# Twenty taps of the depthwise convolution moved to GpSimd, and a sample's rotated keys turned in one flip

## The reference

```
z = rmsnorm(h, ln_in) @ w_in            # c_q, c_kv, k_r, g_a, u_val, u_gate, g_c
s = (q_lat . ckv + q_rope . krope) * ATTN_SCALE        # cached and new keys
o_lat = softmax(s) @ ckv
u = u_val * sigmoid(u_gate)
v = causal_dwconv(concat([past, u]), conv_w, width 31) + bias
v = silu(layernorm(v))
h = h + concat([y_a, y_c]) @ w_out
h = h + sigmoid(rmsnorm(h, ln_pg) @ w_pg) * (p @ w_pe)
```

## Time and profile before

| | |
|---|---|
| median of 3 runs | 798.32 us (798.23 to 798.53) |
| the profiled execution's own time | 798.34 us |
| its span | 796.5 us |
| busy TensorE | 767.9 us |
| busy VectorE | 566.2 us |
| busy ScalarE | 411.7 us |
| busy GpSimd | 65.0 us |

### The profile page before, as it was taken

The page is one execution under the profiler, slowest core; times in us unless marked ns, Lnnn a source line. Parts: engine busy times, 40 slices in busy tenths (PEclk is TensorE's granted clock), DMA queues, the critical chain, the costliest instruction groups (busy, mean ns, idle before and its releaser), DMA issues.

```text
span 796.5 us, 10486 instructions
## 1 busy us (share of the span) xinstructions
PE 767.9 (96%) x3766; PEld 603.7 (76%) x3766; DVE 566.2 (71%) x1093; ACT 411.7 (52%) x942; POOL 65.0 (8%) x114
## 2 busy tenths in 40 slices
PE   6999999999999999999999999999999999999995
PEld 4799877767667578888888988776676756888874
DVE  3348989877877786545463799897878677656477
ACT  3565635654465472353465475457444657323554
POOL 5000123210000220000000011232000000000000
PEclk9999999999999999999999999999999999999998
DMA  8722222100000163422182323211100004341203
GB/s 293 219 72 84 81 69 83 38 27 27 27 1 28 45 206 120 134 80 80 53 259 62 92 88 86 53 57 28 53 14 14 14 14 145 109 144 53 90 17 132
DMA packets 45113, 65.54 MB, mean 82 GB/s; under 512 B 12510, under 2 KB 24634, under 8 KB 45046
## 3 DMA queue, kind: packets, MB, share of 16 engines
q1 hardware_dynamic: 41226, 58.45, 23.3%
q0 software_dynamic: 3776, 6.40, 2.7%
q10 hardware_dynamic: 60, 0.02, 0.0%
HBM read 57.87 MB, written 7.18 MB: 82 GB/s over the span
## 4 chain that ended last, share of the span: by engine, by line
PE 84%; DVE 8%; ACT 5%; issue 2%; DMA 1%; SPq 0%; ACTq 0%; DVEq 0%
PE acc L628 18%; PE acc L630 18%; PE acc L629 18%; PE sharedT L562 4%; PE acc L748 4%; PE sharedT L810 3%; PE sharedS L823 3%; PE sharedO L837 3%; PE sharedS L562 2%; PE sharedO L562 2%; DVE WLO L1379 1%; ACT WHI L1003 1%; DVE VT L1444 1%; PE sharedS L796 1%; PE sharedS L797 1%
## 5 line engine op out<-in xcount | busy, mean ns | idle before, releaser
L628 PE MATMUL acc<-WHI,XHI 128*128 128x512 f32 (+1 forms) x710 | 309.0, 435 | 0.9 <-DVE XLO L1389 0.9
L630 PE MATMUL acc<-WHI,XLO 128*128 128x512 f32 (+1 forms) x710 | 275.3, 388 | 0.0
L629 PE MATMUL acc<-WLO,XHI 128*128 128x512 f32 (+1 forms) x710 | 274.7, 387 | 0.0
L1444 DVE SCALAR_TENSOR_TENSOR VT<-UX,CWT,VT 128x640 f32<-128x640 f32 x240 | 211.8, 883 | 5.4
L628 PEld LDWEIGHTS acc<-WHI,XHI 128*128 128x128 f32 x710 | 133.9, 189 | 33.8 <-issue 8.6
L1379 DVE SCALAR_TENSOR_TENSOR WLO<-WR,GT,WHI 128x512 fp32r<-128x512 f32 (+1 forms) x142 | 98.6, 736 | 82.6 <-ACT WHI L1003 82.2
L629 PEld LDWEIGHTS acc<-WLO,XHI 128*128 128x128 f32 x710 | 134.2, 189 | 30.5 <-issue 8.6
L630 PEld LDWEIGHTS acc<-WHI,XLO 128*128 128x128 f32 x710 | 133.6, 188 | 26.4
L1003 ACT ACTIVATE WHI<-WR,GT 128x512 fp32r<-128x512 f32 (+1 forms) x142 | 93.5, 710 | 95.9 <-PE acc L630 90.9
L1196 ACT ACTIVATE SB<-SB,NBIAS 128x384 f32<-128x384 f32 (+1 forms) x80 | 45.7, 572 | 39.3 <-DVE NBIAS L1500 39.0
L837 PEld LDWEIGHTS sharedO<-V,PT 128*128 128x128 f32 x320 | 44.5, 191 | 16.1 <-issue 8.8
(11 more groups left out here) (207 smaller groups left out, 839.7 us busy)
## 6 DMA issues: line engine op xcount, KB each, us to landing
WR<-in_w_in_dram SPq DMA_DIRECT2D x32, 256.0 KB, 3.0
WR<-in_w_in_dram SPq DMA_DIRECT2D x16, 512.0 KB, 3.7
WR<-in_w_out_dram SPq DMA_DIRECT2D x16, 512.0 KB, 3.6
WR<-in_w_pg_dram SPq DMA_DIRECT2D x16, 512.0 KB, 3.6
WR<-in_w_in_dram SPq DMA_DIRECT2D x8, 416.0 KB, 3.4
residual_spill<-H SPq DMA_DIRECT2D x5, 512.0 KB, 4.1
H<-residual_spill SPq DMA_DIRECT2D x10, 256.0 KB, 3.3
H<-in_x_prompt_dram SPq DMA_DIRECT2D x4, 512.0 KB, 7.6
```

Of the source, the lines that this page charges most:

```text
L628: mm(out, hi, w_hi, start=(first and k == 0), stop=False)
L629: mm(out, hi, w_lo, start=False, stop=False)
L630: last = mm(out, lo, w_hi, start=False, stop=(final and k == 1))
L1444: ins = stt(out=out, in0=src, scalar=w, in1=out, op0=ALU.mult, op1=ALU.add)
```

## The change

Two edits that don't touch each other's data.

The first: of the channel tile c = 3, the taps 0 to 19 leave VectorE's list and go to GpSimd. VectorE keeps 104 taps per layer, 24 of them in the units. GpSimd does tap 0 in one instruction, and each of the other 19 in two, a product into a new tile TAPPED and a sum onto VT; each of them waits for the one before (`conv_pool`). They stand in its list after the SSUM loads and wait for ScalarE's copies of the tile. VectorE's tap (3, 20) waits for all 39 of them. The tuple of taps in the units is a new one, in which the first tap of tile 3 stands in unit 19.

The second: CKR holds the two key blocks side by side in its 128 columns, each twice, so that one flip turns both. `cache_out` copies the latents in one instruction and the two blocks of rotated keys in one each, from 64 partitions to 64 partitions. The zeros stand in CTK from the start instead of in CKR.

```diff
+POOL_TAPS = 20
+TAP_ORDER = [(c, k) for c in range(4) for k in range(TAPS) if c < 3 or k >= POOL_TAPS]
...
-for _u, _m in enumerate((1, 3, 3, 2, 0, 2, 3, 2, 1, 2, 3, 1, 1, 3, 3, 2, 1, 2, 0, 2, 2, 2, 1, 2)):
+for _u, _m in enumerate((0, 1, 1, 1, 0, 1, 1, 1, 1, 1, 1, 1, 1, 1, 1, 0, 0, 0, 0, 2, 2, 2, 2, 3)):
     TAP[NB + _u] = _take(_m)
...
-        CKR = sb("CKR", [P, CACHED, 2, 128])
+        CKR = sb("CKR", [P, CACHED, P])
+        TAPPED = sb("TAPPED", [P, TOK])
...
             src = a["cache_krope"][l, s].rearrange("(j p) r -> p j r", p=P)
+            dst = CKR[:, slot, :].rearrange("p (j k r) -> p k j r", j=2, k=2)
             for k in range(2):
-                lo = NOPE + ROPE * k
-                pool.dma_start(CKR[:, slot, :, lo:lo + ROPE], src).then_inc(cache_in[slot], 16)
+                pool.dma_start(dst[:, k], src).then_inc(cache_in[slot], 16)
...
                 for j in range(2):
                     flip(quad(name)[:, j, :], CKV[:, slot, j, :])
-                    last = flip(quad(name)[:, 2 + j, :], CKR[:, slot, j, :])
-                fill_inc(last, (l, name))
+                fill_inc(flip(quad(name)[:, 2, :], CKR[:, slot, :]), (l, name))
...
-                drain_inc(copy(CTK[:, :, 0:PAST], bank((l, name))[:, :].rearrange("p (a k) -> p a k", a=2)), (l, name))
+                copy(CTK[:, 0, 0:PAST], bank((l, name))[:, 0:PAST])
+                for j in range(2):
+                    out = copy(CTK[NOPE:P, 1, P * j:P * (j + 1)], quad(name)[NOPE * j:NOPE * (j + 1), 2, :])
+                drain_inc(out, (l, name))
...
-                        dve.wait_ge(conv_done, CONVS * l + TAP_AT[c, k - 1] + 1)
+                        if (c, k) == (3, POOL_TAPS):
+                            dve.wait_ge(conv_pool, (2 * POOL_TAPS - 1) * (l + 1))
+                        else:
+                            dve.wait_ge(conv_done, CONVS * l + TAP_AT[c, k - 1] + 1)
...
-            nc.gpsimd.memset(CKR[:, :, :, 0:NOPE], 0.0).then_inc(const_set, 1)
-            nc.gpsimd.memset(CTK[0:NOPE, 1, PAST:], 0.0).then_inc(const_set, 1)
+            nc.gpsimd.memset(CTK[0:NOPE, 1, :], 0.0).then_inc(const_set, 1)
...
+            c, steps = 3, (2 * POOL_TAPS - 1) * l
+            copied_wait(pool, (l, ("u", c, 0)))
+            copied_wait(pool, (l, ("u", c, 1)))
+            out = VTv[:, :, c, :].rearrange("p t (b j) -> p t b j", j=NS)
+            product = TAPPED[:, :].rearrange("p (t b j) -> p t b j", t=TILES, j=NS)
+            for k in range(POOL_TAPS):
+                w = CWT[:, c, k:k + 1]
+                src = UX[:, c % 2, :, k:k + NS].rearrange("p (t b) j -> p t b j", t=TILES)
+                if k == 0:
+                    nc.gpsimd.tensor_scalar(out, src, w, GT[:, l, G_CB + c:G_CB + c + 1],
+                                            ALU.mult, ALU.add).then_inc(conv_pool, 1)
+                else:
+                    pool.wait_ge(conv_pool, steps + 2 * k - 1)
+                    nc.gpsimd.tensor_scalar(product, src, w, None, ALU.mult).then_inc(conv_pool, 1)
+                    pool.wait_ge(conv_pool, steps + 2 * k)
+                    nc.gpsimd.tensor_tensor(out, out, product, ALU.add).then_inc(conv_pool, 1)
```

More of the change, by code:

```diff
@@ L74 @@
          (0, 2), ("x", 3, 1), (1, 1), ("x", 4, 0), (0, 3), ("x", 4, 1), (1, 2), (0, 4), (1, 3), (1, 4)]
-TAP_ORDER = [(c, k) for c in range(4) for k in range(TAPS)]
+POOL_TAPS = 20
+TAP_ORDER = [(c, k) for c in range(4) for k in range(TAPS) if c < 3 or k >= POOL_TAPS]
 TAP_AT = {x: i for i, x in enumerate(TAP_ORDER)}
@@ L293, in build @@
         conv_done = sem("conv_done")
+        conv_pool = sem("conv_pool")
         ln_done = sem("ln_done")
@@ L856, in tensor_layer @@
                 pe.wait_ge(tables_in, 16 * 2)
-                pe.wait_ge(const_set, 10)
+                pe.wait_ge(const_set, 9)
             for t in range(TILES):
@@ L1448, in vector_layer @@
             if l == 0:
-                dve.wait_ge(const_set, 10)
+                dve.wait_ge(const_set, 9)
             taps("z5")
@@ L1752, in pool_start @@
             nc.gpsimd.memset(SMASK[:, 2, 128:240], NEG).then_inc(const_set, 1)
-            nc.gpsimd.memset(CTK[0:NOPE, 1, PAST:], 0.0).then_inc(const_set, 1)
+            nc.gpsimd.memset(CTK[0:NOPE, 1, :], 0.0).then_inc(const_set, 1)
             nc.gpsimd.memset(MASK[:, :], 0.0).then_inc(const_set, 1)
-            pool.wait_ge(const_set, 9)
+            pool.wait_ge(const_set, 8)
             nc.gpsimd.memset(MASK[0:P // 2, 512 - P // 2:512], NEG).then_inc(const_set, 1)
```

## The result

The changed kernel takes 830.11 us (median of 4 runs, 828.94 to 832.13) beside 798.42 us for the kernel before: 4.0% slower, with an interval of the ratio from 1.0379 to 1.042. I had forecast slower, 809.1 us, with a range that ended at 819. The time lies outside it.

The account below looks back on a forecast made before the run. TensorE's own work and short waits were taken to bound the kernel. From 798.34 us, flips -1.5, relief -1.0, third tap +1.6 and blocking +11.7 gave +10.8, so 809.1 us, range 796.5 to 819.

Parts of the forecast that it names:

- What bounds the kernel: Whole kernel: TensorE, busy 96% of the span; time changes only where it has fewer instructions or waits less.
- One flip fewer: Samples' attention: eight flips fewer save 0.88 us per layer, 0.1 lost to ScalarE's copies; -1.5 us in all.
- Relief: Units: VectorE without 20 taps shortens TensorE's waits by 0.5 us per layer, -1.0 us in all.
- the third tap: Unit 23, end of the convolution: three taps instead of two delay TensorE by 0.8 us per layer, +1.6 us.
- The sum of the three terms: Flips -1.5, relief -1.0 and third tap +1.6 together: -0.9 us, giving 797.4 us without disturbance.
- How long GpSimd takes: GpSimd's chain: product 1.0 us, sum 1.6, 54 us per layer (29 to 67), ending at about 223.
- the limit at 62: Units: GpSimd's chain may take 62 us from its start, to about 231, before VectorE's tap (3, 20) is held up.
- GpSimd late: Rival at tap (3, 20): without blocking, the chain ends at 236 and VectorE stands 5 us; 807.4 us, chance 0.08.
- Blocking: Units: GpSimd's reads hold up VectorE's low parts and a gate, 5.85 us per layer, +11.7 us; chance 0.52.
- the four low parts: Units, 169 to 229 us: two VectorE instructions each, before masks for which TensorE's scores already wait; 0.65 us per instruction.
- the lateness: Tap (3, 20): a GpSimd chain late under blocking, nothing in the sum, up to 5 us per layer for the range.
- the slot: When VectorE reaches tap (3, 20): 228.87, moved by blocked low parts to 232.8, with slack 234.8.

Follow-up runs that it names:

- e9: One-flip edit alone on the kernel before, first scores matmul waiting for the latents' copy only, sample 5's probabilities copied before the gate tiles: 796.86 us, ratio 0.9973.
- e12: Kernel before with only ScalarE's order in sample 5 changed, probabilities copied before the gate tiles: 797.81 us, ratio 0.9986.
- e4: Changed kernel, VectorE not waiting for GpSimd (its 11 taps of tile 3 kept apart, not added), GpSimd doing tap 0 alone: 799.69 us, ratio 1.0007.
- e3: Changed kernel, VectorE not waiting for GpSimd (its 11 taps of tile 3 kept apart, not added), GpSimd's work the same: 813.96 us, ratio 1.0191.
- e5: Changed kernel without VectorE's wait, GpSimd's 38 products and sums per layer replaced by 100 dependent memsets: 800.52 us, ratio 1.0018.
- e2: Changed kernel with GpSimd's product written as multiply, then add 0, instead of multiply alone: 817.44 us, ratio 1.0232.
- e11: Kernel before plus 32 dependent GpSimd instructions on idle tiles in the first layer, four of each form; instructions timed, no kernel time given.

## Why the prediction was wrong

- **What bounds the kernel:** right. TensorE's own work and its short waits set the time, and the loss is found again in TensorE's waits and the clock. The waits listed under the result grew by 28.8 us, the clock costs 2.7, the flips give 1.8 back: 29.7 of 30.6 us between the two profiled executions.
- **One flip fewer, -1.5 us:** TensorE does save about 0.88 per layer (scores of the later samples start 5.36 us apart instead of 5.49), but the price of the copies was mis-sized: 1.1 us per layer instead of 0.1. I looked only at the wait for the copies and took for granted that the others were ahead. In sample 5 ScalarE has no gap from the cache copy to the probabilities, so what the copies take more in front is waited for behind, with the flip saved coming on top. Net +0.2 per layer, and -0.58 once the waits are mended (e9 against e12).
- **Relief, -1.0, and the third tap, +1.6:** the third tap measured 0.8 us per layer (L568, 1.6 in two waits). The units, from their first scores to the first flip of the convolution, take 82.8 us in the kernel before (162.03 to 244.82) and in e4 (163.71 to 246.54), although e4 has 0.73 us of wait for that tap. So relief was worth as much, 0.7 per layer where I took 0.5. The sum of the three terms, -0.9 us, was right within what can be measured (e4). That is partly luck, as it has errors of both signs in it: the flips gave nothing and relief gave more.
- **How long GpSimd takes:** here the prediction failed. "I take 1.0 and 1.6": the sum measured 1.53 undisturbed, the product 1.88, outside my bounds of 0.65 to 1.3. The bound rested on a memset and on the thought that streams pass one after another at its rate; that an instruction with less to do can take twice as long isn't in any row. The chain was 74.8 us instead of 54, with the limit at 62 (the 1.59 us per instruction there include the 0.1 between two).
- **The rival "GpSimd late"** (chance 0.08) is what happened: VectorE stood 12.3 us at tap (3, 20). I priced it at 5 us per layer without blocking. It came with blocking, and the two work together: by the runs, about 20.7 us for the length of the instructions, about 11.0 for what the chain grows beside VectorE's instructions.
- **Blocking, +11.7:** the mechanism is there, shown by e3 against e4 (14.3 us), and e5 binds it to what a memset doesn't do. Its size was too small even for durations as I had taken them. e2 comes near the case that I had described: its product and sum take 1.03 and 1.75 us on average, beside my 1.0 and 1.6, its chain ends at 225.8 and nothing waits for it. It takes 817.4 us, 8 us above my 809.1. In the changed kernel the waits behind the four low parts grew by 3.1 us per layer (0.46, 0.81, 1.13 and 0.74), where I had 5.85, and they are hidden in front of the longer wait, since the end of GpSimd's chain sets unit 19. The Trainium skill's rule (SBUF — State Buffer, Who interferes with whom), that a VectorE instruction with two SBUF inputs collides with a GpSimd instruction that reads SBUF and not with one that only writes it, agrees with the changed kernel, e3 and e5: masks keep their length, low parts and taps don't, memsets disturb nothing.
- **Two readings of the rows:** TensorE's scores did not already wait behind all four low parts. Behind the one at 207.25 the kernel before had 0.05 us. And the new tuple doesn't take a tap from every unit: units 8, 11 and 12 keep their one, with the low part in unit 11.
- **The clock:** not in my sum. It cost about 1.4 us per layer behind the long wait, and 3.3 us in the first layer of e2.
- **The range** was too narrow because it took the lateness as a remainder ("up to 5 us per layer") on top of a chain that just fit. By my own sums the chain with blocking ended at 232 to 241 and the slot lay at 232.8 to 234.8, and of this only 2 us per layer went into the range. A wrong duration multiplied by 19 should have carried it.

## What to carry to other kernels

A chain of dependent instructions on an engine that the trace has never shown computing should be timed before it is built around: one wrong duration times its count decides, and once another engine stands for its end, the time follows it nearly microsecond by microsecond. In this kernel elementwise work on GpSimd wasn't free beside VectorE instructions that read two SBUF tensors, so put it where those have room, and none of them in front of a wait of TensorE. When an engine's copy is split, follow its whole list up to its next gap: the cost lands on whatever is behind it, and may sit several samples away.

## What was not expected of the hardware

GpSimd's tensor_scalar over 128x640 float32 took 1.81 to 1.89 us with one operation and 0.80 with two, alike for contiguous elements and windows; a copy took 0.72 to 0.75, a sum of two tensors 1.55 to 1.57, a memset 0.63 (e11, its first two rounds, but for one product of 2.24). VectorE's low part of two instructions (1.41 us) took up to 3.21 us beside GpSimd's shorter products, more than beside the longer ones (up to 2.70). Why isn't settled: that GpSimd takes more turns in the same time would do it, and wasn't tried by itself.

In e11 a small VectorE instruction with one SBUF tensor was long as well. It took 1.53 us where it takes 0.17 in the kernel before, and lies within GpSimd's sum (32.68 to 34.23):

```profile
32.72 1.53 DVE L360 TENSOR_SCALAR NR<-MS 128x5 f32<-128x5 f32 x1 [1.37 <-ACT JUNK L1000]
```

This one case suggests that two SBUF inputs are not the only way to be held up; no experiment was made on it.
